# Products of two feed-forward stages issued as two of 256 columns in place of one of 512

## The reference, cut to what matters

```python
D_MODEL = 1024
SEQ = 256
D_FF = 7 * D_MODEL // 2          # 3584
N_EXPERTS = 8

def swiglu(x, w_gate, w_up, w_down):
    return (jax.nn.silu(x @ w_gate) * (x @ w_up)) @ w_down

def moe_ffn(x, router_w, w_gate, w_up, w_down):
    ...
    for e in range(N_EXPERTS):
        out = out + combine[..., e:e + 1] * swiglu(x, w_gate[e], w_up[e], w_down[e]).astype(F32)
```

## Time and profile before

| what | value |
|---|---|
| median of 3 runs | 1824.55 us (1822.7 to 1826.91) |
| span of the profiled execution, first to last instruction | 1822.6 us |
| median minus that span | 1.95 us |
| PE busy | 1692.0 us (93%) |
| PEld busy | 1379.2 us (76%) |
| DVE busy | 1331.4 us (73%) |
| ACT busy | 947.7 us (52%) |
| DMA, mean | 241 GB/s |
| mean granted clock of TensorE | 0.959 |

### The profile page before, as it was taken

One profiled execution on the slowest core, in us unless ns is written; L12 is line 12 of the kernel. 1 busy time (PEld: TensorE's weight loads), 2 busy tenths in 40 slices (PEclk: granted clock), 3 DMA queues, 4 the chain that ended last, 5 costly groups with the idle time before them and its releaser, 6 DMA issues.

```text
span 1822.6 us, 21422 instructions
## 1 busy us (share of the span) xinstructions
PE 1692.0 (93%) x7990; PEld 1379.2 (76%) x7990; DVE 1331.4 (73%) x1231; ACT 947.7 (52%) x798; POOL 199.3 (11%) x175
## 2 busy tenths in 40 slices
PE   7977969999989789699999999999999999999996
PEld 6856748888878577478878788788788788787885
DVE  7777455445437764658888888888788888888887
ACT  1242114443302421257677677677677776776773
POOL 0343058000003440400000000000000000000000
PEclk9988979999989889789999999999999999999998
DMA  8330035555423200459999899899899899898991
GB/s 307 137 116 1 1 139 181 196 197 189 173 95 124 111 1 6 157 191 374 335 323 374 321 338 373 307 363 373 291 370 363 306 375 354 316 376 321 345 373 67
DMA packets 183976, 440.12 MB, mean 241 GB/s; under 512 B 6577, under 2 KB 8753, under 8 KB 183153
## 3 DMA queue, kind: packets, MB, share of 16 engines
q1 hardware_dynamic: 182640, 431.15, 65.6%
q0 software_dynamic: 1280, 8.24, 1.2%
HBM read 438.32 MB, written 1.05 MB: 241 GB/s over the span
## 4 chain that ended last, share of the span: by engine, by line
PE 80%; DVE 12%; ACT 4%; issue 3%; DMA 1%; DVEq 0%; SPq 0%
PE ps L1344 39%; PE ps L1353 20%; PE ps L1286 5%; PE ps L1594 3%; PE ps L1310 2%; PE ps L1369 2%; ACT hi L567 1%; PE ps L1558 1%; DVE arena L1031 1%; PE ps L1568 1%; PE ps L1293 1%; PE ps L1567 1%; PE ps L1392 1%; DVE x L915 1%; DVE x L911 1%
## 5 line engine op out<-in xcount | busy, mean ns | idle before, releaser
L928 DVE TENSOR_TENSOR lo<-arena,hi 128x2048 fp32r<-128x2048 f32 x372 | 856.6, 2304 | 258.6 <-ACT hi L567 258.5
L567 ACT ACTIVATE hi<-arena 128x2048 fp32r<-128x2048 f32 x378 | 724.5, 1920 | 423.4 <-PE ps L1344 294.8
L1344 PE MATMUL ps<-hi,xg 128*128 128x512 f32 x1792 | 558.6, 393 | 1.5 <-DVE xg L941 1.5
L1344 PEld LDWEIGHTS ps<-hi,xg 128*128 128x128 f32 x1792 | 337.9, 190 | 71.6 <-issue 1.7
L1344 PE MATMUL ps<-lo,xg 128*128 128x512 f32 x896 | 350.8, 392 | 0.0
L1353 PE MATMUL ps<-hi,hTe 128*128 128x512 f32 x896 | 282.5, 396 | 0.7
L1344 PEld LDWEIGHTS ps<-lo,xg 128*128 128x128 f32 x896 | 169.5, 189 | 36.1
L1353 PEld LDWEIGHTS ps<-hi,hTe 128*128 128x128 f32 x896 | 164.0, 188 | 33.4 <-issue 1.6
L1353 PE MATMUL ps<-lo,hTe 128*128 128x512 f32 x448 | 175.0, 391 | 0.0
L1344 PE MATMUL ps<-hi,xs 128*128 128x512 f32 x448 | 140.3, 395 | 2.1 <-DVE xs L1186 2.1
L1286 PE MATMUL ps<-arena 128*128 128x256 f32 x544 | 122.5, 388 | 3.9 <-DMA arena<-in_w_in 2.8
(11 more groups left out here) (326 smaller groups left out, 1715.6 us busy)
## 6 DMA issues: line engine op xcount, KB each, us to landing
arena<-in_mg SPq DMA_DIRECT2D x112, 1024.0 KB, 5.2
arena<-in_mu SPq DMA_DIRECT2D x112, 1024.0 KB, 5.3
arena<-in_md SPq DMA_DIRECT2D x112, 1024.0 KB, 5.0
arena<-in_w_in SPq DMA_DIRECT2D x8, 2048.0 KB, 10.2
arena<-in_wg SPq DMA_DIRECT2D x14, 1024.0 KB, 5.1
arena<-in_wu SPq DMA_DIRECT2D x14, 1024.0 KB, 5.1
arena<-in_wd SPq DMA_DIRECT2D x14, 1024.0 KB, 5.0
arena<-in_w_out SPq DMA_DIRECT2D x4, 2048.0 KB, 7.8
```

The lines of the kernel that those rows point to most:

```text
L567: af(hi[r % PARTS][:, :], raw[r % RAWS], ACT.Copy).then_inc(hi_ready, 1)
L928: tt(lo[r % PARTS][:, :], raw[r % RAWS], hi[r % PARTS][:, :].bitcast(F32), ALU.subtract)\
L1344: ins = mm(ps[:, bank + b, :], tok[a][:, kk * nt + b * P:kk * nt + (b + 1) * P], tiles_of(part[r % PARTS], r)[:, k, :], start=(kk == 0 and ...
```

## The change

A product of the feed-forward stages that neither opens nor closes its sum is issued as two matmuls with the same stationary block: one on columns 0 to 255 of the moving operand and of the PSUM bank, and one on columns 256 to 511. Products that open or close a sum stay whole, since they carry the start and stop flags for the bank. Nothing is changed on the other engines, in the waits or in the transfers.

```diff
+            def runs(whole):
+
+                return (slice(0, 512),) if whole else (slice(0, T), slice(T, 512))
+
...
                                 for n, (a, part) in enumerate(PRODUCTS):
-                                    ins = mm(ps[:, bank + b, :], tok[a][:, kk * nt + b * P:kk * nt + (b + 1) * P],
-                                             tiles_of(part[r % PARTS], r)[:, k, :], start=(kk == 0 and n == 0),
-                                             stop=(kk == KT - 1 and n == 2))
+                                    first, final = kk == 0 and n == 0, kk == KT - 1 and n == 2
+                                    for f in runs(first or final):
+                                        ins = mm(ps[:, bank + b, f],
+                                                 tok[a][:, kk * nt + b * P:kk * nt + (b + 1) * P],
+                                                 tiles_of(part[r % PARTS], r)[:, k, f], start=first, stop=final)
...
                                     for n, (a, part) in enumerate(PRODUCTS):
-                                        ins = mm(ps[:, 2 * b + c, :], hT[j % 2][a][:, h0:h0 + P],
-                                                 tiles_of(part[r % PARTS], r)[:, q, 512 * c:512 * (c + 1)],
-                                                 start=(j == 0 and p == 0 and q == 0 and n == 0),
-                                                 stop=(j == FC - 1 and p == 1 and q == 1 and n == 2))
+                                        first = j == 0 and p == 0 and q == 0 and n == 0
+                                        final = j == FC - 1 and p == 1 and q == 1 and n == 2
+                                        for f in runs(first or final):
+                                            ins = mm(ps[:, 2 * b + c, f], hT[j % 2][a][:, h0:h0 + P],
+                                                     tiles_of(part[r % PARTS], r)[:, q, 512 * c:512 * (c + 1)][:, f],
+                                                     start=first, stop=final)
```

## The result

The changed kernel takes 1923.09 us in the median (1922.08 to 1925.18, 4 runs) against 1825.73 of the kernel before: ratio 1.0541, 95% interval 1.0526 to 1.0556, +97.4 us. It is slower, as forecast, but by eight times the +12 us of the sum, and outside the range of 1810 to 1888 us.

A forecast was written before the change was run, and what follows sets the result against it. The prediction took the distance between product starts on TensorE as the bound; 8 us for splits plus 4 us for code made 12 on a 1822.6 us span, with 1.95 us to the median 1836 us, range 1810 to 1888.

The forecast's parts named there:

- the sum: Whole kernel: 8 us for dearer pairs plus 4 us for code, +12 us on a span of 1822.6.
- The bound: Dense stage and experts: the distance between product starts on TensorE bounds the kernel, 5040 products, 1143 us of 1823.
- The price of a pair: Split feed-forward products: two of 256 columns cost 228.7 ns against 226.7 to 227, +1.7 ns a split.
- the line: Float32r products: stream time interpolated between 58 ns at 128 columns and 227 at 512, giving 114.3 ns at 256.
- rival 2: Split products: a fixed cost each, or loads and streams disturbing each other; pair 240.7 ns, 1889 us, chance 0.13.
- The term of +8 us: Dense stage and experts: 4720 splits at 1.7 ns each.
- The float32 rows: Float32 products, 216 ns at 256 columns and 436 at 512: cutting the moving operand costs hardly anything in itself.
- The load as a lower bound: Split products: two loads of the stationary block keep a pair at 223 ns or more, -4 ns a split, -19 us.
- Rival 1: Split products: the load is the only limit, the 256-column stream hides below it; pair 223 ns, 1805 us, chance 0.18.
- The code: Expert loop: a longer turn may not be kept, so seven returns wait for a packet; +4 us, bounds 0 and 20.
- the cover: Return to the loop's top: the scatter's eight products, 3.49 us at half clock, may cover much of the code wait.
- rival 3: Expert loop: code brought again each turn, TensorE waiting at more packets; 1897 us, 1852 with returns alone; beyond 15 us 0.12.

The follow-up runs named there:

- mixed run: Kernel before with expert products cut to mixed widths, part of the sums left out; no kernel time, a 512, 512, 128 pattern takes 0.575 us.
- after_unrolled: The changed kernel with TensorE's eight expert turns written out in place of the loop: 1875.11 us against 1824.52 of the kernel before, ratio 1.0280.
- before_unrolled: The kernel before with TensorE's eight expert turns written out in place of the loop: 1821.53 us, ratio 0.9983.
- padded kernels: Kernel before, products whole, with waits long reached added behind expert products: 1743, 1827 and 1911 instructions a turn took 1825.33, 1872.42 and 1874.21 us.
- gate_up_only: The changed kernel with only gate and up products split, down products whole: 1942.23 us, ratio 1.0646 to the kernel before.

## Why the prediction was wrong, step by step

**The bound.** Right in the main. TensorE's distance between starts is what reaches the end, and 4720 splits and as many loads were counted right; VectorE's busy time is the same to 0.1 us. "With nothing to hide it" was a little too strong: in the experts 12.6 ns of busy time a split became 11.4 of length, because PE's waits for VectorE shrank.

**The price of a pair: the step that failed first.** "Thus a float32r product of 128 columns needs no more than about 58 ns of TensorE when its weights are there." The condition did not hold for the row. The load of the second product had begun at 902.19 with the first product, and takes 111 ns by the same group; the second product is recorded as started 54 to 58 ns on, before that load is over. So the distance from one recorded start to the very next is no measure of what a product costs. The mixed run shows it: 0.06 us to the next start, 0.121 us of cost. How long a stream of 128 columns really takes no run tells, since the load's 110 ns decide there. With that point gone the line has no lower end, and what remained was the reading the prediction gave to rival 2, columns/2.4 + 13.7 ns: 120.4, measured 120.0. The term of +8 us measures 51 to 54 (after_unrolled over before, and over before_unrolled), 10.7 to 11.4 ns a split, and 12.6 in the dense stage alone. The distance between starts at full clock, 240 against 227, gives 13.3.

The float32 rows misled as support: there a product of 256 columns costs 216 ns, 2.7 over 512/2.4, and cutting is free. Of the two types here, only float32r has a share of 13 ns beyond the columns. TensorE: Matmul & The Clock Gate in the Trainium skill, section Back-to-back issue gap, has 2.5 ns for it, as the gap of a single isolated matmul; in the runs float32r has 11 ns more than that, at 256 and at 512 columns.

**The load as a lower bound.** Right: 110 to 112 ns in stretches of 64, of 128 and of 192 columns. Rival 1 asked for a stream below it, and falls.

**The code: the second step that failed.** The mechanism was in the text, its size was not: "Bounds are 0 and 7 x 2.8 = 20 us", taken at +4. Measured: 48.0 us by the unrolled loop, 6.9 us a return; 49 and 51 us in the padded kernels. The bound came from idle time of other engines, and nothing in the trace of before showed what they waited for or that TensorE's wait would be as short; the branch's own row has 6.5 us. Why it takes this long, with the weight transfers at about 90% share beside it, wasn't tested. And the cover that the text hoped for, the scatter's products, hides only about 1 us: the branch at 1066.4 is followed by the last scatter product at 1067.4. The half clock behind the idle time was not in the sum at all; it is the likely source of the 1.3 us of busy time that a return adds. The prediction's 2096 instructions a turn are products and loads alone; 2183 is the whole number, which changes nothing in its argument.

Runtime: NRT & Kernel Launch in the Trainium skill, section Instruction fetch mechanics, has room for 2048 instructions on TensorE. Here 1743 a turn are kept and 1827 are not, though both are under 2048, so the measurement decides against that number as the limit for a loop. Seven blocks of 256 are 1792, which would fit if a turn may not use the last block; whether its length counts or the number of blocks that it touches, the runs don't separate. The same section says that crossing a block in order is mostly hidden, and the unrolled kernels bear this out.

**The range.** Rival 2 came true, and of rival 3 the wait at the return, at 6.9 us and not 2.8; waits at other packets of a turn did not occur: in the loop PE is idle for issue at the seven returns alone. Each rival alone, 1889 and up to 1897, was just beyond the range, but they are independent and add up; the text treated them as alternatives. 11.9 us in the dense stage, 472 x 8 x 11.4 = 43 in the experts and 48 at the returns make 103; less the 3 us that the loop cost the kernel before too it is 100, against 97.4 measured. The last 3 us are not explained.

## What to carry to other kernels

Read what a short matmul costs from a lasting series, or from a cycle that contains it; the distance to the very next start can be half of it, as 0.06 against 0.121 us here. Before anything is added to the body of a loop on TensorE, count its instructions, two for each product and the waits: somewhere between 1743 and 1827 a turn began to cost 7 us a return here, and 11 us of waiting with the top of the loop where gate_up_only had it, while the same code written out costs nothing. Costs of separate mechanisms that each "may occur" belong in the range as a sum.

## What the runs showed that was not expected

The step at a return: 84 instructions more, from 1743 to 1827, cost 47 to 49 us. The place of the loop's top in the code is worth 32 us by itself. A float32r product costs 120 ns at 256 columns, 147 at 320, 203 at 448 and 227 at 512, and 110 to 112 at anything from 64 to 192.
